# The order of an exponential and two bank copies in ScalarE's attention program

## The reference

```python
def diff_attention(q, k, v, lam):
    # out = (softmax(q1 k1^T/sqrt d) - lam * softmax(q2 k2^T/sqrt d)) v, causal
    ...
        s = jnp.where(mask, s, NEG_BIG)
        p = jax.nn.softmax(s, axis=-1)
        w = p[:, :, 0] - lam * p[:, :, 1]
        return jnp.einsum('bhqk,bhke->bhqe', w.astype(vh.dtype), vh)
```

## Time and profile before

| | |
|---|---|
| median of three runs | 1264.01 us (1263.21 to 1264.35) |
| the profiled execution's own time | 1263.58 us |
| its span, first to last instruction | 1261.8 us |
| TensorE (PE) busy | 1238.1 us, 98% |
| VectorE (DVE) busy | 939.6 us, 74% |
| ScalarE (ACT) busy | 554.9 us, 44% |
| GpSimd (POOL) busy | 145.6 us, 12% |
| attention turns | about 77 to 345 us of the span |

### The profile page before, as it was taken

The page is one execution under the profiler, slowest core; times in us unless marked ns, Lnnn a source line. Parts: engine busy times, 40 slices in busy tenths (PEclk is TensorE's granted clock), DMA queues, the critical chain, the costliest instruction groups (busy, mean ns, idle before and its releaser), DMA issues.

```text
span 1261.8 us, 16103 instructions
## 1 busy us (share of the span) xinstructions
PE 1238.1 (98%) x5865; PEld 1020.2 (81%) x5865; DVE 939.6 (74%) x1314; ACT 554.9 (44%) x957; POOL 145.6 (12%) x197
## 2 busy tenths in 40 slices
PE   6999999998999999999999999999999999999998
PEld 5877877787878888888887888888888888888887
DVE  5547785767997679764578777777778998879764
ACT  5436665656654323322345445345354433333330
POOL 2113322322400040000000000000000000000034
PEclk9999999999999999999999999999999999999999
DMA  8100120111365466422214543544569644262333
GB/s 288 34 17 14 43 71 18 42 35 55 131 238 187 154 213 217 166 101 84 107 45 142 175 148 137 175 143 141 175 210 364 228 165 167 100 233 101 100 100 134
DMA packets 109632, 170.27 MB, mean 135 GB/s; under 512 B 5725, under 2 KB 55538, under 8 KB 109554
## 3 DMA queue, kind: packets, MB, share of 16 engines
q1 hardware_dynamic: 109554, 169.25, 38.9%
HBM read 118.89 MB, written 50.33 MB: 134 GB/s over the span
## 4 chain that ended last, share of the span: by engine, by line
PE 86%; DVE 8%; ACT 3%; issue 2%; DMA 0%; SPq 0%; ACTq 0%; DVEq 0%
PE bank L2213 80%; PE bank L2353 2%; PE bank L2334 1%; DVE small L1528 1%; PE bank L2293 1%; DVE slot_lo L1446 1%; PE bank L2284 1%; DVE w_tok L1546 1%; DVE c L2122 1%; DVE pair_lo L2016 1%; DVE wT_lo L1512 1%; PE bank L2531 1%; DMA raw<-in_w_in 0%; ACT prob L1032 0%; PE bank L2231 0%
## 5 line engine op out<-in xcount | busy, mean ns | idle before, releaser
L2213 PE MATMUL bank<-o_hi,s_hi 128*128 128x512 f32 x448 | 174.5, 390 | 0.0
L2213 PE MATMUL bank<-o_hi,s_lo 128*128 128x512 f32 x448 | 174.5, 389 | 0.0
L2122 DVE TENSOR_TENSOR c<-bank,c 128x512 f32<-128x512 f32 x112 | 75.7, 689 | 35.5 <-PE bank L2213 33.9
L2213 PE MATMUL bank<-featT_hi,pair_hi 128*128 128x512 f32 x256 | 100.0, 391 | 0.8 <-DVE c L2122 0.7
L2213 PE MATMUL bank<-featT_lo,pair_hi 128*128 128x512 f32 x256 | 99.7, 390 | 0.0
L2213 PE MATMUL bank<-o_lo,s_hi 128*128 128x512 f32 x256 | 99.7, 390 | 0.0
L2213 PE MATMUL bank<-featT_hi,pair_lo 128*128 128x512 f32 x256 | 99.7, 389 | 0.0
L2213 PEld LDWEIGHTS bank<-o_hi,s_lo 128*128 128x128 f32 x448 | 84.1, 188 | 17.5
L2213 PEld LDWEIGHTS bank<-o_hi,s_hi 128*128 128x128 f32 x448 | 84.1, 188 | 17.3
L1414 ACT ACTIVATE s_hi<-s_raw 128x2048 fp32r<-128x2048 f32 x28 | 53.7, 1917 | 95.5 <-DMA s_raw<-u_store 95.5
L1390 ACT ACTIVATE c<-c 128x512 f32<-128x512 f32 x64 | 39.9, 624 | 118.9 <-DVE c L2122 118.9
(11 more groups left out here) (263 smaller groups left out, 3160.9 us busy)
## 6 DMA issues: line engine op xcount, KB each, us to landing
s_raw<-u_store SPq DMA_DIRECT2D x28, 1024.0 KB, 5.6
pair_raw<-in_w_mlp_in SPq DMA_DIRECT2D x16, 1024.0 KB, 5.8
u_store<-s_tile SPq DMA_DIRECT2D x64, 256.0 KB, 2.1
o_raw<-in_w_mlp_out SPq DMA_DIRECT2D x16, 1024.0 KB, 8.0
u_store<-u_tile SPq DMA_DIRECT2D x48, 256.0 KB, 2.4
gate_store<-out_tile SPq DMA_DIRECT2D x32, 256.0 KB, 2.0
gate_raw<-in_w_in SPq DMA_DIRECT2D x8, 1024.0 KB, 5.4
raw<-in_w_in SPq DMA_DIRECT2D x12, 512.0 KB, 4.8
```

The lines of the kernel that those rows point to most:

```text
L2122: nc.vector.tensor_tensor(out[:], psum, other[:], ALU.add).then_inc(up_sum, 1)
L2213: mm = nc.tensor.matmul(out, a, b, start=start and i == 0, stop=stop and i == len(steps) - 1, skip_group_check=onto)
```

## The change

The second exponential of a row is issued right behind the first, and `output_part`, the two copies out of the bank OUT, behind both. Waits and semaphores are as before, and the programs of the other engines are unchanged.

```diff
@@ -1113,10 +1113,10 @@
                     weights_hi(g - W_LAG, 0)
                 if g < ROWS:
                     exponential(0, g)
+                if g < ROWS:
+                    exponential(1, g)
                 if rows_at(g, O_LAG) or rows_at(g, N_LAG):
                     output_part(g - O_LAG)
-                if g < ROWS:
-                    exponential(1, g)
                 if rows_at(g, SUM_LAG):
                     output_norm(g - SUM_LAG)
                 if rows_at(g, O_LAG):
```

## The result

| | before | after |
|---|---|---|
| median | 1264.17 us | 1272.62 us |
| lowest and highest of six runs each | 1263.21, 1264.40 | 1269.95, 1274.11 |
| the profiled execution | 1263.58 us | 1269.95 us |
| its span | 1261.8 us | 1268.2 us |
| mean granted clock of the six runs | | 0.996 to 0.998 |

The ratio is 1.0064, with a 95% interval from 1.0054 to 1.0075: the change makes the kernel 8 us slower. The profiled execution is where the sum of the prediction put it (1270.0), and the median is 2.2 us above the forecast of 1270.4. The runs before lie within 1.2 us of each other, those after within 4.2.

A forecast was written before the change was run, and what follows sets the result against it. TensorE, busy 98% of the span, was taken as the bound, so only its waits count. Terms 3.55 + 2.04 + 0.8 = 6.4 us gave 1270.0 for the profiled execution, 1270.4 as forecast median, range 1265.6 to 1273.5.

The forecast's parts named there:

- The direction and the bound: Attention stage: the change pays or costs only where TensorE waits for other engines; slower by over 2.5 us, chance 0.83.
- The ScalarE part: Copies go behind the second exponential, which starts 0.33 to 0.41 us earlier; the copies come 0.87 to 1.09 later.
- The VectorE part: output_sum waits for the later copies, delaying coefficients, weights and wT_lo: 1.16 us in turn 14, 0.46 in turn 15.
- Output_square: On ScalarE it waits for the later output_sum: 0.43 us later in turn 11, 0.47 in turn 13.
- The sum: Delays add up from turn to turn in the attention stage: 6.4 us in total; chance 0.70.
- its large terms: Long-row stretches: turns 11 to 15 together 3.55 us, turns 28 to 30 together 2.04 us.
- The small terms: Later qk_norm awaited by TensorE's transpose in turns 8 (0.34 us) and 22 (0.45 us), together 0.8 us.
- No accumulation: Rival: each late row is taken back, only each stretch's largest delay stays; 3.0 us, 1267; chance 0.13.
- faster: Rival: transposing two turns later covers VectorE's delay, so exponential waits shrink by 2.2 us; 1261.1; chance 0.05.
- not effective: Rival: copies wait for TensorE's outputs past the second exponential anyway; 1264; chance 0.08.
- The clock: Rival: clock falls to 1.2 GHz at turn 15's transpose, some 20 slower matmuls cost 4.6 us; 1275; chance 0.04.

The follow-up runs named there:

- The failed experiment: Against the kernel after: output_sum moved behind the weights of the same turn on VectorE, output_square left in its place; 1293.34 us, ratio 1.0231.
- the trace without falls of the clock: Kernel after with eight unread matmuls ahead of the transposes of turns 13, 15 and 29 and six more in turn 16; 1270.35 us, ratio 1.0049.
- the second trace of the kernel after: Profiled execution of the kernel after, run once more with no edit; 1272.62 us, in a series with median 1273.28 us, ratio 1.0067.
- The eleven runs: All executions of the unedited kernel after, the six of the result and those of its repetition; 1269.7 to 1274.1 us.
- x5: Kernel after with eight matmuls that nobody reads ahead of the transposes of turns 13, 15 and 29; 1272.21 us, ratio 1.0065.
- x8: Kernel after with TensorE's first two pieces of fill ahead of the transpose of queries and keys in turns 13, 15 and 29; 1269.94 us, ratio 1.0044.
- x7: Kernel after with output_square moved to the next turn on ScalarE and output_sum behind the weights on VectorE; 1267.78 us, ratio 1.0027.
- x6: Kernel after with output_square moved to the next turn on ScalarE, ahead of wT_hi; 1269.28 us, ratio 1.0045.

## Why the prediction was right, and where it was off

**The direction and the bound.** Right. TensorE's waits decide, and only in the long turns.

**The ScalarE part.** Right in sign. The second exponential now starts 0.12 us behind the start of the first's accumulator read (181.02 to 181.14), and five of the six waits of TensorE for an exponential have gone. Nothing was won by it, as TensorE waits longer at the transpose instead: 2.6 us less at L2334, 4.4 more at L2284, whose 7.6 us stay under the forecast of some 10. The distance from start to start was the right price of the copies: after the change they take 0.40 us (182.25 to 182.65), not half of their 0.64.

**The VectorE part.** Right and nearly exact: 1.16 forecast, 1.14 measured in turn 14. The sum of VectorE's waits for the copies is 29 us where over 20 were forecast, but 9 of them were there before. The run with qk_norm first shows that this wait is the cause.

**Output_square.** The mechanism was right. Its price in the sum (0.9 us in turns 11 and 13) is lower than what moving it gives back, 1.5 us to turn 15. The prediction counted the wait in two turns with a weight split behind it and left out a third, turn 7, whose split in turn 8 is held back in the same way. The failed experiment shows how much weight lies on this arm.

**The sum.** Right to a tenth, as the trace without falls of the clock shows, and its large terms hold one by one. From mask to mask turns 11 to 15 add 0.44, 0.99, 0.44, 1.10 and 0.45 (forecast 0.43, 1.03, 0.47, 1.16, 0.46), turns 28 to 30 add 1.00, 0.42 and 0.48 (1.04, 0.47, 0.53). To turn 15 it gives 4.02 us, where 3.55 and 0.34 (turn 8) were forecast; by turn 27 it is 4.45, 0.43 more, where turn 22 was put at 0.45; turns 28 to 31 give 1.9 for 2.04. Together 6.36, against 6.4. The small terms are right in size by luck. Turn 8 was put down to a qk_norm 1.19 us late, a delay taken from the long turn 14; in the even turns alone it is 0.79 late (50.54 to 51.33 from the first scores) and its transpose is not late at all, while turn 7, which the sum left out, brings about half a microsecond. Of the 0.4 us at turn 22, too, about half are seen in the odd turns alone. The even and the odd turns by themselves show that the terms add up.

**No accumulation, faster, not effective.** None of the three happened: the delay rises step by step, the time is higher, and the two exponentials do stand side by side.

**The clock: the step that was mis-sized.** The prediction had it as a rival, with a chance of 0.04 and 4.6 us for a fall in turn 15. In truth it is no alternative to the sum but comes on top of it, in both traces of the kernel after, and costs 0.4 us where it falls in turn 13 and 1.6 in turn 15 or 16. The size was too high because I let 20 matmuls fall under it, a number that no row gave; at 0.43 us apart 3.4 us hold 8, which lose 1.6. The chance was too low for two reasons. The attention stage before has no wait of TensorE's matmuls over 1.3 us, so its full clock says nothing about stalls of 2. And the argument that the row of the clock is full even in the first slice was wrong: there 9 matmuls are 0.43 us apart behind 8 us of idle time, and the row does not show it.

How the forecast was passed by 2.2 us can be read in the second trace of the kernel after, whose time (1272.62) is that of the median. It is 9.04 us longer than the profiled execution of before: 6.36 are the order, 1.60 the clock (7.96 in the table), 1.04 the later start (78.99 against 77.95). So in this execution the clock has the larger part of what the sum lacks and the start the rest. For the median itself that stays likely and not shown. The eleven runs order themselves by their clock, and the kernel without falls has 1270.35; but the runs of x5 and x8 do not order themselves so, and only two of the eleven have a trace. The width of the range covered both; neither was in the sum.

The Trainium skill (TensorE: Matmul & The Clock Gate, Part 1) has the clock fall after idle time, and says that the point of a change varies from run to run. The second half agrees with the runs: the same kernel showed the fall in turn 13 in one execution and in turn 15 in another. The length of the last wait alone does not decide here: the clock fell behind a wait of 0.93 us in turn 16 and stayed full behind one of 1.96.

## What to carry to other kernels

Before an instruction is moved back in an in-order queue, look at who waits for it, what stands behind that wait in the other engine's queue, and what stands behind the wait that follows from it: here a copy of 0.3 us held back maxima, weights and transposes through an addition of 0.3 us. Move the consumer along with it, in all the queues of the chain, or leave the order alone; moving one queue alone cost 8 us, moving two of them 29, and moving all of them, in even turns only, 1.2, or nothing with a piece of TensorE's work moved too. And where stalls of TensorE grow beyond the longest that the trace has, count with a lower clock after them, read it from the distance of equal matmuls as well as from the row of the clock, and take several executions before a difference of 2 us is explained.

## What the runs showed of the hardware that was not expected

- The granted clock fell to 0.5 for some 3.4 us after stalls of 1.96 and 2.08 us in the middle of busy work, in two kernels (x5, x8) in turn 16 after one of 0.93, and in x7 there after one of 1.54. It did not fall after two other stalls of 1.96 us in the first trace of the kernel after, nor after one of 2.07 us in x6.
- Where it falls differs between executions of one kernel. In turns 15 and 16 it cost 1.6 us, in turn 13, partly under a wait for the other engines, 0.4.
- The first matmuls of 512 columns run 0.43 us apart instead of 0.23 behind 8 us of idle time, 9 of them before and 6 or 12 in the two traces of the kernel after, and the row of the granted clock says 1.00 there. The time to the first scores, before any part of the change runs, differs between executions, from 77.6 to 79.3 us, and most of the difference stands by 18 us.
